# The output projection of a hybrid mixer block: three products of rounded and residual parts in place of one fp32 product

## The chip, the cores and the metric

The kernel runs on one core of a Trainium2 chip. The metric is the device time of one execution in microseconds. The inputs are fp32, and so is the output.

## What is computed

One block of a network over 512 rows of width 1024: a norm, a mixer, a residual; a second norm, a mixture of 32 experts, a residual. Cut to what matters here:

```
merged = g_sb * (y_sb @ w_o_sb) + g_rw * (y_rw @ w_o_rw)      # [512, 1024]
y  = merged @ w_out                                           # w_out [1024, 1024]
x  = x + gt1 * rmsnorm(y, norm_gains[l, 1])                   # x1
h  = rmsnorm(x, norm_gains[l, 2]) * (1.0 + sc2) + sh2
group_logits, expert_logits = h @ w_group, h @ w_router       # two experts a row
y  = sum over e of combine[:, e] * ((silu(h @ w_up1[e]) * (h @ w_up3[e])) @ w_down[e])
```

The change is in the second line, `merged @ w_out`.

## The kernel before, in words

Each engine has its own instruction stream, written out by hand, and the streams meet at counting semaphores. There is no planner: the order of the work is the order of the calls. All of SyncE's DMAs are on one queue. The work falls into stages:

- **Up to 544 us of the profile.** Modulation rows, the input projection, attention and the recurrent mixer. The first 15 tiles of the input projection (L1484 to L1486) are already computed as three products of rounded upper parts and lower parts in the type fp32r. Their upper parts are made by ScalarE (L661 for the weights, L673 for the rows), their lower parts by GpSimd (L520, L528) and VectorE (L1013).
- **Merging, 544 to 573.** TensorE makes eight tiles of the recurrent branch, each from four fp32 products (L1809, `mix_done`). VectorE multiplies each by its gate (L1199) and adds it to `merged` (L1200, `merged_ready`). `merged` is [128, 8, 512]: piece k holds 128 of the 1024 inner columns of all 512 rows, and lies in the first third of `ring`.
- **Output projection, 573 to 634.** `w_out` is loaded in two halves of 512 columns, WO1 first (into arena tiles 6 and 7), then WO0 (into the second third of `ring`). For each half TensorE goes over four tiles of 128 rows (t), each a sum over k of eight fp32 products 128x128 by 128x512: L1837 for WO1, L1847 for WO0, 32 products each. An fp32 product is two matmul records in the trace. A tile that is finished raises `y_done`. In the second half the transposes of finished rows (`transposes_x1`, L1819) and their router logits (`router_logits`, L1827) stand between the products of later tiles.
- **Behind each tile.** ScalarE squares and sums it (L866 for the first half, L870 for the second), takes the root (L872, L873), squares the row `x1` (L879 to L881), moves the transposed rows (L884), scales the row (L889) and stores it to DRAM (L890, `h2_stored`). VectorE makes `x1` (L1258, L1260, L1261, `x1_ready`). Ahead of the fourth tile of the second half VectorE also chooses experts for the first 256 rows (`choose(0)`, L1220 to L1248).
- **Routing, 634 to 661.** The last transposes and logits, the choice for the other rows, ranks and indices on VectorE with short products on TensorE, and some fp32 filler products (L1852). GpSimd then gathers the rows of the first experts (L563, `idx_ready`, `hrow_in`).
- **Experts, 661 to 1140.** 32 experts and some overflow blocks, 6 MB of weights each. Three sets of buffers are filled in turn by SyncE (L388 for `up`, L392 and L396 for `down`). Ahead of the loop, SyncE's list goes: at `merged_ready` = 8 it loads `down` of set 0 and, at `mix_done` = 32, both halves of `up` of set 1; at `y_done` = 4 `down` of set 1; at `y_done` = 8 both halves of `up` of set 0; at `x1_ready` = 8 one part of set 2 (L458, L459); and after `hrow_in[0]`, the landing of the first gather, the other part of set 2 (L464, L465), with which the loop follows. Each `load_expert(u, 0 or 1, e)` is two DMAs of 1 MB.

`S(i, n)` is n tiles of 2048 elements from tile i of the arena. `hT`, the transposed input rows, is S(15, 2), and is read last by the gate products ahead of 544.

Of the kernel before, what the change touches and what calls it, by code (L numbers as in the profile page):

```python
# [13 lines left out]
F32 = mybir.dt.float32  # L14
F32R = mybir.dt.float32r
I32 = mybir.dt.int32
ALU = mybir.AluOpType
# [3 lines left out]
P = 128  # L21
# [96 lines left out]
def build(nc, x, c, w_mod, b_mod, gains, w_in, gate_bias, shift_mu, w0, w_decay_up, a0, w_iclr_up, w_gate_up,  # L118
# [3 lines left out]
    with ctx:  # L122
        def sb(name, shape, dt=F32):
            return ctx.enter_context(nc.sbuf_tensor(name, shape, dt))
# [14 lines left out]
        with (nc.sbuf_tensor("w_parts", [P, 2, 2, KD, P], F32R) as w_parts,  # L139
              nc.sbuf_tensor("between0", [P, 2 * 4096 + 3 * 2048], F32), nc.sbuf_tensor("h_upper", [P, KD, T], F32R) as h_hi,  # L140
              nc.sbuf_tensor("between1", [P, 2048], F32), nc.sbuf_tensor("h_lower", [P, KD, T], F32R) as h_lo):
            pass
        ring = sb("ring", [P, 3, 4096])

        with nc.sbuf_tensor("below", [P, 10 * 2048], F32), nc.sbuf_tensor("sp_parts", [P, 4, ZW], F32R) as sp_parts:
# [29 lines left out]
        def S(i, n=1):  # L175
            return arena[:, i:i + n, :].rearrange("p a b -> p (a b)")
# [38 lines left out]
        acc_l += [rt[:, :], S(12, 1)[:, 1024:1536], S(12, 1)[:, 1536:2048]]  # L215

        y_late = S(2, 1).rearrange("p (t n) -> p t n", t=NT)
        y_early = S(13, 1)[:, 0:1024].rearrange("p (b n) -> p b n", b=2)
        squares = S(12, 1)[:, 1024:2048]
        shift_wr = rt[:, 0:KD * (NG + E)].rearrange("p (k n) -> p k n", k=KD)  # L220
        shift_row = rt[:, 470:470 + NG + E]
        h2tok = S(5, 1).rearrange("p (b n) -> p b n", b=2)
# [141 lines left out]
        def arrived(eng, name):  # L364

            n = chunk_names.index(name)
            eng.wait_ge(ring_in[slot_of[n]], 16 * slot_of[:n + 1].count(slot_of[n]))
# [44 lines left out]
        def _(sp):  # L412
# [32 lines left out]
            load_expert(sp, 0, 2, 0)  # L445
            sp.wait_ge(mix_done, 4 * KD)
            load_expert(sp, 1, 0, 1)
            load_expert(sp, 1, 1, 1)
            sp.wait_ge(y_done, NT)
            load_expert(sp, 1, 2, 1)  # L450
            sp.wait_ge(y_done, 2 * NT)
            load_expert(sp, 0, 0, 0)
            load_expert(sp, 0, 1, 0)
            first = lambda i, m: esrc[i][:, bass.ds(2, 1), 2048 * m:2048 * m + 2048].rearrange("p a n -> p (a n)")
            first_down = dn[:, bass.ds(2, 1), :, :].rearrange("p a k n -> p (a k) n")
            sp.wait_ge(x1_ready, 2 * NT)
# [59 lines left out]
        def _(pool):  # L516
# [32 lines left out]
            for n in range(KD):  # L549
                pool.wait_ge(osb_evac, n + 1)  # L550
                nc.gpsimd.tensor_tensor(merged[:, n, :], merged[:, n, :], osb[:, n % 2, :], ALU.mult).then_inc(sb_gated, 1)

            pool.wait_ge(merged_ready, KD)
            nc.gpsimd.memset(S(14), 0.0)
            nc.gpsimd.memset(S(13)[:, D:2 * D], 0.0).then_inc(hrow_zero, 1)
# [57 lines left out]
        def _(act):  # L613
# [246 lines left out]
            gate_evac(6)  # L860
            gate_evac(7)
            nc.scalar.preload_act_table_set("natural_log_exp_and_others")

            for t in range(NT):
                act.wait_ge(y_done, t + 1)
# [81 lines left out]
        def _(dve):  # L947
# [244 lines left out]
            ins.then_inc(yrw_ready, 1)  # L1192
            dve.wait_ge(yrw_ready, 1)

            dve.wait_ge(sb_gated, KD)
            for n in range(KD):
                dve.wait_ge(gr_evac, max(n + 1, 6))
                dve.wait_ge(mix_done, 3 * KD + n + 1)
                link(TT(gated[:, n % 2, :], gates_rw[:, n, :], ps[:, n % 4, :], ALU.mult))  # L1199
                TT(merged[:, n, :], merged[:, n, :], gated[:, n % 2, :], ALU.add).then_inc(merged_ready, 1)  # L1200
            dve.wait_ge(rows_moved, 80)
            dve.wait_ge(x_in, 32)
            for t in range(NT):
# [46 lines left out]
            for t in range(NT):  # L1250
                if t == NT - 1:
                    dve.wait_ge(rstd2, 2)
                    logits_out(0)
                    link(logits_out(1))
                    choose(0)
                dve.wait_ge(half_squared, NT + t + 1)
                y = y_early[:, t % 2, :]
                link(TT(y, ps[:, 4 + t, :], rows[:, 0, 0:512], ALU.mult))  # L1258
                dve.wait_ge(rstd1, t + 1)
                STT(x1[:, t, 512:1024], y_late[:, t, :], V("rs", 4 + t), x1[:, t, 512:1024], ALU.mult, ALU.add).then_inc(x1_ready, 1)  # L1260
                STT(x1[:, t, 0:512], y, V("rs", 4 + t), x1[:, t, 0:512], ALU.mult, ALU.add).then_inc(x1_ready, 1)  # L1261
# [135 lines left out]
        def _(pe):  # L1397
# [431 lines left out]
                last.then_inc(logit_done, 1)  # L1829


            pe.wait_ge(merged_ready, KD)
            arrived(pe, "WO1")
            for t in range(NT):
                w = chunk("WO1", KD)
                for k in range(KD):
                    last = mm(ps[:, t, :], merged[:, k, P * t:P * t + P], w[:, k, :], start=(k == 0), stop=(k == KD - 1))  # L1837
                last.then_inc(y_done, 1)
            arrived(pe, "WO0")
            for t in range(NT):  # L1840
                w = chunk("WO0", KD)
                for k in range(KD):
                    if k == 2 and t >= 2:
                        router_logits(t - 2)
                    if k == 4 and t >= 1:
                        transposes_x1(t - 1)
                    last = mm(ps[:, 4 + t, :], merged[:, k, P * t:P * t + P], w[:, k, :], start=(k == 0), stop=(k == KD - 1))  # L1847
                last.then_inc(y_done, 1)
            def idle_products(count):

                for _ in range(count):
                    mm(ps[:, 1, :], K("ones"), cst[:, 0:512], start=True, stop=True, skip_group_check=True)  # L1852
# [134 lines left out]
```

## Time and profile before

| | us |
|---|---|
| median of 3 runs | 1174.03 (1172.61 to 1175.0) |
| profiled execution, its own time | 1173.3 |
| its span, first to last instruction | 1171.1 |
| TensorE busy | 1034.2 (88%) |
| VectorE, ScalarE, GpSimd busy | 384.3, 259.9, 170.7 |
| mean granted TensorE clock | 0.975 |
| moved by DMA | 281.64 MB, mean 240 GB/s |

The durations in the rows come from the one profiled execution. Times in the rows are us from the first instruction, or ns where a group gives a mean. "PE" is TensorE's products, "PEld" its loads of the stationary operand, DVE is VectorE, ACT ScalarE, POOL GpSimd and SPq the queue that SyncE issues. Matmul ends are modelled, so the distance from start to start is what a product costs, and not the duration of one record. The granted clock is 1.00 at 2.4 GHz and 0.50 at 1.2 GHz.

### The profile page before, as it was taken

Reading aid. Unit: us, or ns where it says so; the run is one execution under the profiler, and the core shown is the slowest. Engines: PE = TensorE matmul, PEld = TensorE weight load, DVE = VectorE, ACT = ScalarE, POOL = GpSimd, SP = SyncE. Lnnn points to the kernel's source line nnn. Section 1 sums busy time; section 2 is a strip of 40 time slices with the busy share of each in tenths; the row PEclk is TensorE's granted clock in tenths of the full one; section 3 lists DMA queues with packets and bytes.
Section 4 is the critical chain, followed back from the end, with each engine's and each line's share of the span. In section 5 each row is a group of like instructions: output and inputs, shape, how many; then the busy total and the mean of one; then the engine's idle time right before and its main releaser. Section 6 shows DMA issues by size and latency. Waiting matters only on the chain.

```text
span 1171.1 us, 16601 instructions
## 1 busy us (share of the span) xinstructions
PE 1034.2 (88%) x6906; PEld 516.8 (44%) x6906; DVE 384.3 (33%) x810; ACT 259.9 (22%) x407; POOL 170.7 (15%) x222
## 2 busy tenths in 40 slices
PE   3899999999998999999999799987778777887886
PEld 1578644466555676544446333332233332332231
DVE  1322566465547442114215521221111111111114
ACT  2342350075552222233024000000000000000004
POOL 0345100003320100000100112111111111011002
PEclk9699999999999999999999899999999999899998
DMA  8444304443321002325334899999999999999995
GB/s 327 151 135 134 130 14 143 144 144 109 108 82 63 3 4 76 109 76 213 154 133 169 313 400 403 401 391 411 406 404 409 406 406 409 392 399 401 412 412 224
DMA packets 71184, 281.64 MB, mean 240 GB/s; under 512 B 9754, under 2 KB 19244, under 8 KB 46554
## 3 DMA queue, kind: packets, MB, share of 16 engines
q1 hardware_dynamic: 63408, 265.94, 58.7%
q0 software_dynamic: 5120, 8.40, 2.2%
q10 hardware_dynamic: 2602, 6.52, 1.5%
q8 instruction: 42, 0.69, 0.2%
q14 instruction: 12, 0.10, 0.0%
HBM read 276.62 MB, written 12.60 MB: 247 GB/s over the span
## 4 chain that ended last, share of the span: by engine, by line
PE 51%; SPq 30%; DMA 7%; DVE 5%; ACT 4%; issue 2%; POOL 1%; ACTq 0%; POOLq 0%; DVEq 0%
SPq L388 21%; PE ps L1590 7%; SPq L392 5%; PE ps L1471 5%; PE ps L1901 4%; SPq L396 3%; PE ps L1601 2%; PE ps L1484 2%; DMA ring<-in_w_up 2%; PE ps L1485 2%; PE ps L1486 2%; PE ps L1837 2%; PE ps L1847 2%; PE ps L1809 2%; PE ps L1516 2%
## 5 line engine op out<-in xcount | busy, mean ns | idle before, releaser
L1901 PE MATMUL ps<-arena 128*64 128x512 f32 x672 | 151.7, 596 | 31.9 <-DMA arena<-in_w_up 31.9
L1357 DVE TENSOR_TENSOR arena<-arena,ps 128x256 f32<-128x256 f32 x32 | 13.5, 421 | 372.1 <-ACT arena L904 372.1
L1590 PE MATMUL ps<-arena,ring 128*128 128x512 f32 x256 | 118.6, 604 | 0.2 <-DMA ring<-in_w_in 0.2
L1901 PEld LDWEIGHTS ps<-arena 128*64 128x64 f32 x672 | 48.6, 137 | 133.4 <-issue 101.9
L1916 PE MATMUL ps<-arena 128*64 128x512 f32 x336 | 79.9, 618 | 20.0 <-DMA arena<-in_w_down 15.3
L1901 PE MATMUL ps<-ring,arena 128*64 128x512 f32 x352 | 80.5, 603 | 18.9 <-DMA ring<-in_w_up 18.7
L904 ACT ACTIVATE arena<-ps 128x256 f32<-128x256 f32 x32 | 12.3, 383 | 260.9 <-PE ps L1901 260.9
L1590 PEld LDWEIGHTS ps<-arena,ring 128*128 128x128 f32 x256 | 46.1, 190 | 49.0 <-issue 47.2
L1352 DVE TENSOR_SCALAR arena<-ps,par 128x64 f32<-128x64 f32 x256 | 67.1, 333 | 0.5 <-PE ps L1890 0.5
L911 ACT ACTIVATE arena<-ps 128x512 f32<-128x512 f32 x32 | 19.1, 597 | 187.9 <-PE ps L1916 187.9
L536 POOL TENSOR_SCALAR_AFFINE_SELECT arena<-arena 128x128 f32<-128x128 f32 x64 | 32.3, 537 | 186.4 <-DVE arena L1092 168.6
L1901 PEld LDWEIGHTS ps<-ring,arena 128*64 128x64 f32 x352 | 24.2, 138 | 74.2 <-issue 42.1
L1916 PE MATMUL ps<-ring,arena 128*64 128x512 f32 x176 | 46.7, 680 | 10.7 <-DMA ring<-in_w_down 8.3
L1471 PE MATMUL ps<-arena,ring 128*128 128x512 f32 x128 | 55.1, 592 | 0.0
L1916 PEld LDWEIGHTS ps<-arena 128*64 128x64 f32 x336 | 25.5, 142 | 60.0 <-issue 43.0
L1484 PE MATMUL ps<-h_upper,w_parts 128*128 128x512 f32 (+1 forms) x120 | 47.9, 399 | 4.4 <-ACT arena L669 4.4
L520 POOL TENSOR_TENSOR w_parts<-ring,w_parts 128x1024 fp32r<-128x1024 f32 (+1 forms) x15 | 38.6, 2577 | 79.8 <-ACT w_parts L661 79.8
L589 POOL COPY dst_now<-dst_i 128x1 int32 x27 | 4.8, 177 | 300.2 <-ACT arena L911 300.2
L1485 PE MATMUL ps<-h_lower,w_parts 128*128 128x512 f32 (+1 forms) x120 | 47.7, 398 | 0.0
L1486 PE MATMUL ps<-h_upper,w_parts 128*128 128x512 f32 (+1 forms) x120 | 47.6, 397 | 0.0
L1890 PEld LDWEIGHTS ps<-cst,arena 64*128 64x128 f32 x256 | 30.7, 200 | 28.5 <-issue 28.5
L1471 PEld LDWEIGHTS ps<-arena,ring 128*128 128x128 f32 x128 | 24.3, 190 | 30.6 <-issue 30.6
(354 smaller groups left out, 1472.2 us busy)
## 6 DMA issues: line engine op xcount, KB each, us to landing
arena<-in_w_up SPq DMA_DIRECT2D x84, 1024.0 KB, 28.8
ring<-in_w_up SPq DMA_DIRECT2D x44, 1024.0 KB, 28.5
ring<-in_w_down SPq DMA_DIRECT2D x11, 2048.0 KB, 34.8
arena<-in_w_down SPq DMA_DIRECT2D x11, 2048.0 KB, 32.1
ring<-in_w_mod SPq DMA_DIRECT2D x10, 2048.0 KB, 9.1
arena<-in_w_down SPq DMA_DIRECT2D x20, 1024.0 KB, 28.2
ring<-in_w_in SPq DMA_DIRECT2D x6, 2048.0 KB, 8.4
ring<-in_w_in SPq DMA_DIRECT2D x8, 1024.0 KB, 9.0
```

The costliest lines, as they stand in the source:

```text
L388: eng.dma_start(eset_up[u][i][:, 2048 * m:2048 * m + 2048], src).then_inc(w_in_sem[u][m], 16)
L392: eng.dma_start(dst, src).then_inc(w_in_sem[u][m], 16)
L396: eng.dma_start(eset_down[u][i], src[:, i, :]).then_inc(w_in_sem[u][m], 16)
L520: nc.gpsimd.tensor_tensor(w_parts[:, n % 2, 1, :, 0:w], chunk(name, KD)[:, :, a:a + w], w_parts[:, n % 2, 0, :, 0:w].bitcast(F32), ALU.sub ...
L1352: last = TS(hgT[:, k, :], ps[:, 0, CAP * k:CAP * k + CAP], V("A1", k), V("SH1", k), ALU.mult, ALU.add)
L1471: last = mm(ps[0:m_, b, :], w[:, k, a:a + m_], hT[:, k, :], start=(k == 0), stop=(k == KD - 1))
L1484: mm(ps[0:m_, b, :], hi, h_hi[:, k, :], start=(k == 0), stop=False)
L1485: mm(ps[0:m_, b, :], hi, h_lo[:, k, :], start=False, stop=False)
L1486: last = mm(ps[0:m_, b, :], lo, h_hi[:, k, :], start=False, stop=(k == KD - 1))
L1590: last = mm(ps[:, bank, :], w[:, k, P * (n % 2):P * (n % 2) + P], hT[:, k, :], start=(k == 0), stop=(k == KD - 1))
L1901: last = mm(ps[64 * hf:64 * hf + 64, UP_BANK[u], :].rearrange("p (m n) -> p m n", m=2), hgT[:, k, :], up_pair(u, k)[:, :, 256 * hf:256 * h ...
L1916: last = mm(ps[64 * hf:64 * hf + 64, DOWN_BANK[u], :], hv2[:, k % 2, k // 2, :], wd[:, k % 2, 512 * hf:512 * hf + 512], start=(k == 0), st ...
```

## The change

The 64 fp32 products of the output projection become 192 products of the type fp32r: for each piece k and each row tile, upper part of `merged` by upper part of `w_out`, lower part of `merged` by upper part of `w_out`, upper part of `merged` by lower part of `w_out`. ScalarE makes the upper parts (a copy to fp32r), GpSimd the lower parts of the weights, VectorE those of `merged`. The lower parts overwrite what they come from. The upper parts of WO1 lie in `hT`, those of WO0 in arena tiles 9 and 11, those of `merged` in tiles 0, 1 and 13. Tiles 9 and 11 are the second half of `up` of set 1, so its load goes behind `y_done` = 8. TensorE no longer waits for all of `merged` ahead of the first product, but for each piece's parts in the first row tile of each half. Lines of the diff that only declare are kept where the text speaks of them.

```diff
@@ build: storage (element counts per partition, 4 bytes each)
+        with (nc.sbuf_tensor("over0", [P, 4096], F32), nc.sbuf_tensor("wo0_lower", [P, KD, 512], F32R) as wo0_lower,
+              nc.sbuf_tensor("over1", [P, 4096 + 1024], F32), nc.sbuf_tensor("m_upper0", [P, 6, 512], F32R) as m_upper0,
+              nc.sbuf_tensor("over2", [P, 7 * 2048], F32), nc.sbuf_tensor("wo0_upper0", [P, 4, 512], F32R) as wo0_upper0,
+              nc.sbuf_tensor("over3", [P, 2048], F32), nc.sbuf_tensor("wo0_upper1", [P, 4, 512], F32R) as wo0_upper1,
+              nc.sbuf_tensor("over4", [P, 2048], F32), nc.sbuf_tensor("m_upper1", [P, 2, 512], F32R) as m_upper1,
+              nc.sbuf_tensor("over5", [P, 3072], F32), nc.sbuf_tensor("wo1_upper", [P, KD, 512], F32R) as wo1_upper):
+            pass
-        y_early = S(13, 1)[:, 0:1024].rearrange("p (b n) -> p b n", b=2)
+        y_early = [a[:, :, :].rearrange("p b n -> p (b n)") for a in (SAs, SDZ)]
+        m_hi = [m_upper0[:, k, :] for k in range(6)] + [m_upper1[:, k, :] for k in range(2)]
+        m_lo = [w_parts[:, :, :, :, :].rearrange("p a b k n -> p (a b k n)")[:, 512 * k:512 * k + 512] for k in range(KD)]
+        wo_hi = [[wo1_upper[:, k, :] for k in range(KD)],
+                 [wo0_upper0[:, k, :] for k in range(4)] + [wo0_upper1[:, k, :] for k in range(4)]]
+        wo_lo = [[h_lo[:, k, :] for k in range(KD)], [wo0_lower[:, k, :] for k in range(KD)]]
@@ block.sync
             load_expert(sp, 1, 0, 1)
-            load_expert(sp, 1, 1, 1)
             sp.wait_ge(y_done, NT)
             load_expert(sp, 1, 2, 1)
             sp.wait_ge(y_done, 2 * NT)
             load_expert(sp, 0, 0, 0)
             load_expert(sp, 0, 1, 0)
+            load_expert(sp, 1, 1, 1)
@@ block.gpsimd, ahead of pool.wait_ge(merged_ready, KD)
+            def output_weight_lower(half, k):
+                pool.wait_ge(w_rounded, len(proj_tiles) + KD * half + k + 1)
+                nc.gpsimd.tensor_tensor(wo_lo[half][k], chunk(("WO1", "WO0")[half], KD)[:, k, :], wo_hi[half][k].bitcast(F32), ALU.subtract).then_inc(w_split, 1)
+            for k in range(KD):
+                output_weight_lower(0, k)
+            for k in range(KD):
+                output_weight_lower(1, k)
@@ block.scalar, ahead of the first act.wait_ge(y_done, t + 1)
+            def output_weight_upper(half, k):
+                A(wo_hi[half][k], chunk(("WO1", "WO0")[half], KD)[:, k, :], ACT.Copy).then_inc(w_rounded, 1)
+            arrived(act, "WO1")
+            for k in range(KD):
+                output_weight_upper(0, k)
+                act.wait_ge(merged_ready, k + 1)
+                A(m_hi[k], merged[:, k, :], ACT.Copy).then_inc(h_rounded, 1)
+            arrived(act, "WO0")
+            for k in range(KD):
+                if k == 4:
+                    act.wait_ge(mix_done, 4 * KD)
+                output_weight_upper(1, k)
@@ block.vector, the loop that makes merged
+            def merged_lower(k):
+                dve.wait_ge(h_rounded, KD + k + 1)
+                TT(m_lo[k], merged[:, k, :], m_hi[k].bitcast(F32), ALU.subtract).then_inc(h_split[1], 1)
                 TT(merged[:, n, :], merged[:, n, :], gated[:, n % 2, :], ALU.add).then_inc(merged_ready, 1)
+                if n:
+                    merged_lower(n - 1)
+            merged_lower(KD - 1)
-                y = y_early[:, t % 2, :]
+                y = y_early[t % 2]
@@ block.tensor
-            pe.wait_ge(merged_ready, KD)
-            arrived(pe, "WO1")
+            def output_products(half, t, k):
+                if t == 0:
+                    pe.wait_ge(h_split[1], KD // 2 + k + 1)
+                    pe.wait_ge(w_split, len(proj_tiles) + KD * half + k + 1)
+                at, bank = slice(P * t, P * t + P), 4 * half + t
+                mm(ps[:, bank, :], m_hi[k][:, at], wo_hi[half][k], start=(k == 0), stop=False)
+                mm(ps[:, bank, :], m_lo[k][:, at], wo_hi[half][k], start=False, stop=False)
+                return mm(ps[:, bank, :], m_hi[k][:, at], wo_lo[half][k], start=False, stop=(k == KD - 1))
             for t in range(NT):
-                w = chunk("WO1", KD)
+                pe.wait_ge(merged_ready, KD // 2 + t + 1)
                 for k in range(KD):
-                    last = mm(ps[:, t, :], merged[:, k, P * t:P * t + P], w[:, k, :], start=(k == 0), stop=(k == KD - 1))
+                    last = output_products(0, t, k)
                 last.then_inc(y_done, 1)
-            arrived(pe, "WO0")
             for t in range(NT):
-                w = chunk("WO0", KD)
                 for k in range(KD):
                     if k == 2 and t >= 2:
                         router_logits(t - 2)
                     if k == 4 and t >= 1:
                         transposes_x1(t - 1)
-                    last = mm(ps[:, 4 + t, :], merged[:, k, P * t:P * t + P], w[:, k, :], start=(k == 0), stop=(k == KD - 1))
+                    last = output_products(1, t, k)
                 last.then_inc(y_done, 1)
```

## Rows read from the trace of the kernel before

**Rows 1.** The page, part 2: 40 slices of 29.3 us each.

```profile
PE   3899999999998999999999799987778777887886
...
PEclk9699999999999999999999899999999999899998
DMA  8444304443321002325334899999999999999995
```

**Rows 2.** The chain that ended last: start us, us, what.

```profile
543.99 27.48 PE ps L1809 x64
573.03 27.73 PE ps L1837 x64
...
657.09 3.70 DMA arena<-h_rows,idx_i
...
1096.42 28.21 DMA ring<-in_w_up
```

**Rows 3.** Timeline, 572 to 601: start us, us, engine, line, operation.

```profile
573.03 27.73 PE L1837 MATMUL ps<-arena,ring 128*128 128x512 f32 x64 [1.57 <-DVE ring L1200]
...
573.57 0.19 PEld L1837 LDWEIGHTS ps<-arena,ring 128*128 128x128 f32 x1 [0.24 <-issue]
...
600.18 0.19 PEld L1847 LDWEIGHTS ps<-ring 128*128 128x128 f32 x1 [0.24 <-issue]
```

**Rows 4.** Timeline of TensorE, 87 to 100: input projection, three products a step.

```profile
87.94 0.39 PE L1486 MATMUL ps<-h_upper,w_parts 128*128 128x512 f32 x1
...
99.50 0.39 PE L1486 MATMUL ps<-h_upper,w_parts 128*128 128x512 f32 x1
```

**Rows 5.** Windows: us, busy time of each engine, granted clock, DMA share, GB/s.

```profile
50.50:54.90 4.40, 4.40 (x11) 3.37 (x11) 1.66 (x3) 0.70 (x2) 1.28 (x1) 0.50 0.00 0
...
650.00:655.00 5.00, 1.60 (x30) 1.60 (x32) 4.51 (x20) 0.00 (x0) 0.00 (x0) 0.76 1.00 423
655.00:660.00 5.00, 4.08 (x12) 1.38 (x8) 4.11 (x17) 0.89 (x1) 2.31 (x3) 0.56 0.16 48
```

**Rows 6.** Groups by line, whole span, shapes apart: busy, mean ns.

```profile
L1200 DVE TENSOR_TENSOR ring<-ring,arena 128x512 f32<-128x512 f32 x8 | 5.5, 691 | 0.3
...
L528 POOL TENSOR_TENSOR h_lower<-arena,h_upper 128x512 fp32r<-128x512 f32 x4 | 5.2, 1302 | 4.1 <-ACT h_upper L673 4.1
...
L673 ACT ACTIVATE h_upper<-arena 128x512 fp32r<-128x512 f32 x8 | 4.6, 622 | 0.1
```

**Rows 7.** Timeline, 47 to 49: VectorE and GpSimd side by side.

```profile
47.07 1.39 POOL L528 TENSOR_TENSOR h_lower<-arena,h_upper 128x512 fp32r<-128x512 f32 x1 [0.58 <-ACT h_upper L673]
...
47.54 1.47 DVE L1013 TENSOR_TENSOR h_lower<-arena,h_upper 128x512 fp32r<-128x512 f32 x1 [0.20 <-ACT h_upper L673]
```

**Rows 8.** Timeline, 607 to 636: the second half's products, and what follows them.

```profile
607.67 0.60 ACT L870 ACTIVATE arena<-ps 128x512 f32<-128x512 f32 x1 [5.85 <-PE ps L1847]
...
609.79 0.75 DVE L1261 SCALAR_TENSOR_TENSOR arena<-arena,par 128x512 f32<-128x512 f32 x1
...
614.25 0.35 ACTq L890 DMA_DIRECT2D h_rows<-arena  x1
...
628.37 0.26 DVE L1220 SCALAR_TENSOR_TENSOR arena<-ps,par,rt 128x36 f32<-128x36 f32 x1 [0.40 <-PE ps L1827]
...
633.48 0.23 DVE L1248 TENSOR_TENSOR arena<-arena 128x64 f32<-128x64 f32 x1
...
634.47 2.11 SPq L388 DMA_DIRECT2D ring<-in_w_up  x4
...
634.47 0.60 ACT L870 ACTIVATE arena<-ps 128x512 f32<-128x512 f32 x1 [1.38 <-PE ps L1847]
...
635.19 0.69 DVE L1258 TENSOR_TENSOR arena<-ps,arena 128x512 f32<-128x512 f32 x1 [1.49 <-ACT arena L870]
```

**Rows 9.** Line L563, the gathers of rows: issues and landing.

```profile
L563 POOL DMA_INDIRECT arena<-h_rows,idx_i x5: 936/951/1146, 657.1 to 1082.1; - x5
...
DMA to landing us min/median/max: 3.7/7.2/8.5
```

## The prediction

> **What bounds the kernel now.** I read the slices first. TensorE is busy nearly throughout, and the DMA share lies at 9 tenths from the 24th slice on, while in the 13th to the 22nd it is 5 tenths at most [rows 1]. So the kernel has two parts with different limits. The chain of waits says the same: up to about 650 us it goes through TensorE's products, the output projection's among them, and then over the first gather, which takes 3.70 us, into a long run of weight transfers whose last one lands at 1124.6 [rows 2]. What stands ahead of that run and on the chain moves the end by its full length; what makes the experts' arithmetic faster would not.
>
> At the start of the output projection the timeline shows a wait of 1.57 us: TensorE could begin at 571.46, and begins at 573.03, when the last piece of `merged` is there [rows 3]. Then its loads follow each other without a pause at the full clock: from the third, at 573.57, to the first of the second half, at 600.18, are 62 steps [rows 1, 3].
>
> **Products.** An fp32 product is two records. One record costs (600.18 - 573.57) / 62 = 0.429 us, one product 0.858, and 64 of them 54.9 us [rows 3]. The new form is in the trace already, in the input projection: 51 products of type fp32r, of the same shape, start between 87.94 and 99.50, so one costs 11.56 / 51 = 0.2267 us [rows 4]. 192 of them are 43.5 us. The sum gains **11.4 us**, all on the chain. The 0.39 us that a record shows is its modelled duration, with its neighbours overlapped; the starts decide.
>
> The Trainium skill, "TensorE: Matmul & The Clock Gate", section "Wait — 56ns, not 53.3ns?", gives 215.7 ns from start to start for 512 columns at the warm clock; that would make 192 products 41.4 us and the gain 2.1 us larger. The trace has 226.7 for this very type and shape, and that is used.
>
> **The wait ahead of them.** The new list lets TensorE start once five pieces are merged, and asks for each piece's parts only when it comes to it. It starts at 571.46: **1.6 us** more. Is the last piece ready in time? It is needed after 21 products, at 571.46 + 21 x 0.2267 = 576.2. `merged` is complete at 573.0. ScalarE's rounding takes 0.62 and VectorE's subtraction 0.69 [rows 6], so 574.3. If GpSimd works beside it, a subtraction takes 1.47 in place of 0.69 [rows 7], so 575.1. Both fit, by 1.1 us at least, and I cost it at nothing.
>
> **The weights' parts.** For WO1, ScalarE has 2 x 0.62 us of work per piece of `merged`, and pieces come every 27.48 / 8 = 3.4 us [rows 2, 6]. VectorE's work per piece goes from 1.4 to 2.1 us, or 2.8 beside GpSimd, under the same cover. GpSimd needs 1.30 to 1.39 us each [rows 6, 7]; its eighth starts two roundings behind the seventh merged piece, at 569.6 + 1.2 = 570.8, and ends at 572.2, four microseconds ahead of need. For WO0, ScalarE rounds eight pieces from 573.7 to 578.7; behind them wait only its sums of squares, the first due at 576.9, which has until the second half to be done. GpSimd's eight subtractions, from 574.3 on, end by 574.3 + 11.1 = 585.4. The second half starts at 571.46 + 96 x 0.2267 = 593.2. The cover is 8 us deep; without it 11.1 us would lie on TensorE's path. GpSimd's clearing of buffers, behind these, is not needed before the gather.
>
> **The second half's tiles.** Two chains ran here beside slower products, and must be checked. ScalarE's chain for one tile runs from 607.67 to 614.60, 6.9 us [rows 8]. A tile of products now takes 24 x 0.2267 = 5.4, with about 0.9 of transposes 6.3, and in the last two tiles some 1.7 of router logits on top. So the second tile's sum starts 0.6 late, and this is regained in the third. The transposes come 12 products, 2.7 us, behind a tile, and the rows they need come 2.2 and 2.9 behind it (607.67 to 609.79, and 0.75 more) [rows 8]; the one needed last has four transposes of cover. VectorE's choice for the first rows runs from 628.37 to 633.7, and the first instruction behind it starts at 635.19 [rows 8]: 1.5 us of slack. It is released inside the fourth tile, behind which six pieces are left; they shrink by 6 x (0.858 - 0.680) = 1.1 us. 0.4 us of slack remains. I cost all this at nothing, with a bound of 1.5 us.
>
> So everything from the last tile on comes 11.4 + 1.6 = **13.0 us** earlier.
>
> **The moved load.** Two DMAs of 1 MB leave a place, at 573, where the DMA has time, for the stretch behind the last tile, and on SyncE's queue they stand behind the loads of set 0 and ahead of set 2's and of the wait for the gather. Two more issues delay set 2's by about 1 us, which nobody waits for. At 423 GB/s, 2.1 MB are 5.0 us of stream. The stream from 634.47 on ends near 655 before, and then the DMA is nearly idle until the gather has landed, at 660.8 [rows 2, 5, 8]. The new stream ends 5.0 us later against the stage, near 660; the gather is issued at 657.1, so it falls within the last 2.9 us of it, where it had the DMA for itself. The gather's landing takes 3.7 us in idle DMA (its minimum) and 7.2 in the median, most of them under load [rows 9]. The delay is thus between 0 and 3.5 us. The overlap is about half of what a gather in full load sees, so I take the middle, **1.8 us**. The resumption of the stream waits for that landing, so this is lost at the end as well; the 5.0 us itself is not, since it fills idle time.
>
> By the Trainium skill, "DMA: Bandwidth & Descriptors", section "Queues, rings and completion order", each DMA engine alternates between queues packet by packet. A gather of 64 rows of 4 KB would then take only its own 0.6 us twice, and the sum would be 1.2 us lower. The median landing under load is 3.5 us longer, so more than taking turns stands behind it here.
>
> **The sum.** The profiled execution took 1173.3 us. 1173.3 - 13.0 + 1.8 = 1162.1. It lies 0.7 below the median of the three runs, which spread over 2.4; I put the forecast between the two footings, at **1162.4**.
>
> **Rivals.**
> 1. *The hidden things are not hidden.* The load's move costs the full 3.5, and one of the chains of the second half (ScalarE, choice) or the piecewise start gives 1.5 to 3 us of waits. For it: slacks of 0.4 and 1.1 us are thin, and waits at every piece are new. Against: each was priced with margin. 1173.3 - 13.0 + 3.5 + 1.5 to 3 = 1165.3 to 1166.8. Chance 0.15.
> 2. *The stream absorbs the gain* (no change). If the transfers from 573 on were one unbroken run, an earlier projection would only lengthen a wait further on. Against: the DMA is nearly idle from 655 to 660 [rows 5], and mostly unused during the projection [rows 1]. The time would be 1173 to 1175. Chance 0.05.
> 3. *Slower: the clock.* At half clock ten fp32r products start in 4.40 us, 0.44 each [rows 5], which is more than a third of an fp32 product at full clock. Three products beat one only while their mean is below 0.858 / 3 = 0.286 us, and with the 1.6 and 1.8 counted about the same. If the denser mix of loads and products, or a pause at the first piece, dropped the clock in this stage, 192 x 0.44 = 84.5 us against 54.9: 1173.3 + 29.6 - 1.6 + 1.8 = 1203; at a quarter of the products so slowed, 1173.3 - 11.2 + 48 x 0.213 = 1172, from where it turns. Against: the granted clock is 9 tenths or more in every slice but the second, the later products of this type included, and TensorE comes out of 30 us without a pause [rows 1, 2]. Chance 0.03.
> 4. *The form is not what it says*: fp32r products between these operands run as fp32 ones, 192 x 0.858, and the time is near 1280. The trace has one record for each such product, and a third of the cost [rows 4]. Chance 0.01.
>
> The forecast's own case, 1159.5 to 1164.5, has 0.76. It covers a landing delay of 0 to 3.5 us and both footings.
>
> **The numbers.** The range goes from 1159.0 (no delay, and the run-to-run spread) to 1167.0, the upper end of rival 1, and holds about 0.9; with doubt about my own bookings, 8 in 10. No measurement of this kernel tells a difference under 0.2% (2.3 us) from none. Faster by more: 0.91 (the own case and rival 1), within: 0.05 (rival 2), slower: 0.04 (rivals 3 and 4).
>
> **What the changed profile would show.** The first output product at 571.5 with no wait for VectorE; starts 0.227 us apart, granted clock 1.00; the first half over 21.8 us later, near 593; the last `y_done`, where SyncE issues set 0's `up`, at 621.4 in place of 634.5; the DMA in use without a gap up to the gather; the gather's landing at 5 to 6 us in place of 3.7, and at 648 to 650. From there to the end the same length as before. I would be wrong if products of the first row tiles wait for GpSimd or ScalarE, if VectorE's choice holds the last tile's `x1`, or if the expert stage takes longer than before although it starts earlier.

## The result, and the profile after

| | before | after |
|---|---|---|
| median, us | 1174.13 (1172.61 to 1175.0) | 1162.76 (1162.51 to 1165.32) |
| ratio | | 0.9909, 95% interval 0.9895 to 0.9923 |
| span of the profiled execution | 1171.1 | 1160.9 |
| TensorE busy | 1034.2 | 1021.3 |
| ScalarE, GpSimd busy | 259.9, 170.7 | 273.3, 190.9 |

The time falls by 11.4 us, 1.0%. The forecast was 1162.4, with a range of 1159.0 to 1167.0.

The page's slices, which answer to [rows 1]:

```profile
PE   3799999999998999999998699988787877778785
...
PEclk9799999999999999999999799999999999999999
DMA  9444304443322002315346999999999999999995
```

TensorE has 64 more matmul records and 13 us less work. The DMA's run of nines begins one slice earlier.

The timeline where the projection begins, TensorE first and then the other engines, answers to [rows 3]:

```profile
571.61 0.79 PE L1881 MATMUL ps<-wo_upper,m_upper 128*128 128x512 f32 x1
572.24 0.39 PE L1882 MATMUL ps<-wo_upper,w_parts 128*128 128x512 f32 x1
...
572.70 0.40 PE L1881 MATMUL ps<-wo_upper,m_upper 128*128 128x512 f32 x1
...
579.52 0.39 PE L1881 MATMUL ps<-wo_upper,m_upper 128*128 128x512 f32 x1
```

```profile
573.00 0.69 DVE L1240 TENSOR_TENSOR ring<-ring,arena 128x512 f32<-128x512 f32 x1
...
573.61 1.48 DVE L1233 TENSOR_TENSOR w_parts<-ring,m_upper 128x512 fp32r<-128x512 f32 x2
...
573.73 0.63 ACT L892 ACTIVATE m_upper<-ring 128x512 fp32r<-128x512 f32 x1 [2.28 <-DVE ring L1240]
...
574.27 4.26 ACT L886 ACTIVATE wo_upper<-ring 128x512 fp32r<-128x512 f32 x8
...
574.96 6.30 POOL L568 TENSOR_TENSOR wo_lower<-ring,wo_upper 128x512 fp32r<-128x512 f32 x5 [2.15 <-ACT wo_upper L886]
```

The first product follows the last one of the merging (the stage began 0.7 us later in this execution, which no part of the change touches), with no wait for VectorE. From 572.70 to 579.52 are 30 products: 0.2273 us each, against 0.2267 in [rows 4]. The last piece of `merged` is complete at 573.7, its parts at 575.1 (the two subtractions of VectorE from 573.61 are the seventh and the eighth). TensorE needs them after 21 products, at 576.8 by these starts, and does not stop.

The groups of the new work on the other engines (busy us, mean ns of one), which answer to [rows 6]:

```profile
L568 POOL TENSOR_TENSOR h_lower<-arena,wo_upper 128x512 fp32r<-128x512 f32 x8 | 10.2, 1270 | 108.6 <-ACT wo_upper L886 108.6
L568 POOL TENSOR_TENSOR wo_lower<-ring,wo_upper 128x512 fp32r<-128x512 f32 x8 | 10.0, 1293 | 2.2 <-ACT wo_upper L886 2.2
...
L1233 DVE TENSOR_TENSOR w_parts<-ring,m_upper 128x512 fp32r<-128x512 f32 x8 | 5.5, 684 | 0.1
L892 ACT ACTIVATE m_upper<-ring 128x512 fp32r<-128x512 f32 x8 | 5.0, 630 | 18.3 <-DVE ring L1240 18.3
...
L886 ACT ACTIVATE wo_upper<-ring 128x512 fp32r<-128x512 f32 x8 | 4.3, 616 | 0.0
```

None of it stands on the chain. ScalarE's eight roundings of WO0 follow each other from 574.27, GpSimd's subtractions from 574.96; the second half of the products begins at 594.

SyncE's queue and the first gather, as issues and as a piece of the chain:

```profile
573.72 0.38 SPq L404 DMA_DIRECT2D ring<-in_w_down  x1
...
593.99 0.38 SPq L404 DMA_DIRECT2D arena<-in_w_down  x1
622.11 2.56 SPq L400 DMA_DIRECT2D ring<-in_w_up  x4
624.71 1.30 SPq L400 DMA_DIRECT2D arena<-in_w_up  x2
...
651.60 0.80 SPq L476 DMA_DIRECT2D arena<-in_w_up  x2
...
660.47 4.64 SPq L400 DMA_DIRECT2D ring<-in_w_up  x4
```

```profile
644.74 6.78 DMA arena<-h_rows,idx_i
```

These rows give the stage lengths. SyncE issues at 573.72 when `merged` is complete, at 622.11 when the last output tile is: 48.39 us, where it was 573.01 to 634.47, 61.46 us. That is **13.07 us** less. The gather is issued 22.6 us behind the last tile, as before. Its landing takes 6.78 us against 3.70 [rows 2].

The slack of VectorE's choice and ScalarE's chain, which answer to [rows 8]:

```profile
622.14 0.23 DVE L1291 TENSOR_TENSOR arena<-arena 128x64 f32<-128x64 f32 x1
622.83 0.69 DVE L1301 TENSOR_TENSOR SDZ<-ps,arena 128x512 f32<-128x512 f32 x1 [0.46 <-ACT arena L905]
```

```profile
606.43 0.60 ACT L905 ACTIVATE arena<-ps 128x512 f32<-128x512 f32 x1 [0.43 <-ACT arena L924]
```

The choice ends at 622.37, and the next instruction waits 0.46 us for ScalarE. Only at the second tile does ScalarE go from one tile's chain into the next without waiting for TensorE (0.43 us behind its own last instruction); at the others it waits for the products.

### The profile page after: what moved, and what is told of

It reads as the page before. It is cut to its first block, busy times and chain, and to the rows that moved or that the text cites. A ratio compares the mean times of both kernels' runs of the same rounds, so it can differ in the third digit from the quotient of the medians.

```text
span 1160.9 us, 16792 instructions
## 1 busy us (share of the span) xinstructions
PE 1021.3 (88%) x6970; PEld 533.8 (46%) x6970; DVE 391.0 (34%) x818; ACT 273.3 (24%) x431; POOL 190.9 (16%) x238
## 4 chain that ended last, share of the span: by engine, by line
PE 52%; SPq 28%; DMA 7%; DVE 5%; ACT 4%; issue 2%; POOL 1%; ACTq 0%; POOLq 0%; DVEq 0%
SPq L400 20%; PE ps L1633 7%; SPq L404 5%; PE ps L1514 5%; PE ps L1951 5%; SPq L408 3%; PE ps L1966 3%; PE ps L1644 2%; DMA ring<-in_w_up 2%; PE ps L1527 2%; PE ps L1528 2%; PE ps L1529 2%; PE ps L1559 2%; PE ps L1852 2%; DMA ring<-in_w_mod 2%
## 5 line engine op out<-in xcount | busy, mean ns | idle before, releaser
L1951 PE MATMUL ps<-arena 128*64 128x512 f32 x672 | 151.7, 596 | 33.8 <-DMA arena<-in_w_up 33.8
L1966 PE MATMUL ps<-arena 128*64 128x512 f32 x336 | 83.5, 641 | 19.8 <-DMA arena<-in_w_down 15.1
L1951 PE MATMUL ps<-ring,arena 128*64 128x512 f32 x352 | 81.2, 605 | 17.2 <-DMA ring<-in_w_up 17.2
L1633 PEld LDWEIGHTS ps<-arena,ring 128*128 128x128 f32 x256 | 46.1, 190 | 49.0 <-issue 47.2
L1951 PEld LDWEIGHTS ps<-ring,arena 128*64 128x64 f32 x352 | 26.8, 139 | 70.0 <-issue 39.4
L1966 PE MATMUL ps<-ring,arena 128*64 128x512 f32 x176 | 41.7, 617 | 10.6 <-DMA ring<-in_w_down 8.2
L1940 PE MATMUL ps<-cst,arena 64*128 64x64 f32 x256 | 35.0, 278 | 6.0 <-DMA arena<-h_rows,idx_i 6.0
```

The lines of the kernel that those rows point to most:

```text
L1633: last = mm(ps[:, bank, :], w[:, k, P * (n % 2):P * (n % 2) + P], hT[:, k, :], start=(k == 0), stop=(k == KD - 1))
L1940: last = tr(ps[:, 0, CAP * k:CAP * k + CAP], hv[:, k, :], ident[0:CAP, 0:CAP])
L1951: last = mm(ps[64 * hf:64 * hf + 64, UP_BANK[u], :].rearrange("p (m n) -> p m n", m=2), hgT[:, k, :], up_pair(u, k)[:, :, 256 * hf:256 * h ...
L1966: last = mm(ps[64 * hf:64 * hf + 64, DOWN_BANK[u], :], hv2[:, k % 2, k // 2, :], wd[:, k % 2, 512 * hf:512 * hf + 512], start=(k == 0), st ...
```

## The experiments

All were compared with the kernel before in the same rounds. For each, the table gives the median and five lengths from SyncE's queue and the chain of its profiled execution: from `merged` complete to the last output tile; from there to the issue of the first gather; its landing; from its issue to the first release of a buffer by TensorE (the second time that `up` of set 0 is loaded); and from there to the end of the span.

| | median, us | projection | to gather | landing | issue to release | release to end |
|---|---|---|---|---|---|---|
| before | 1174.13 | 61.46 | 22.62 | 3.70 | 11.99 | 502.0 |
| changed | 1162.76 | 48.39 | 22.63 | 6.78 | 15.73 | 500.4 |
| changed, second job | 1161.74 | 48.39 | 22.63 | 7.47 | 15.87 | 500.7 |
| changed, third job | 1163.55 | 48.36 | 22.64 | 6.83 | 15.64 | 499.9 |
| E1 before, load moved | 1173.73 | 61.45 | 22.65 | 4.95 | 12.65 | 501.3 |
| E2 changed, no gather wait | 1163.62 | 48.41 | 22.61 | 7.92 | 15.86 | 500.4 |
| E3 before, no gather wait | 1178.62 | 61.46 | 22.65 | 8.47 | 16.35 | 500.9 |
| E4 changed, two products | 1152.62 | 36.12 | 25.76 | 3.82 | 11.89 | 501.3 |
| E5 changed, waits for all of `merged` | 1164.55 | 50.25 | 22.64 | 6.64 | 14.19 | 501.5 |
| E6 changed, 1 MB left early | 1160.26 | 48.38 | 22.62 | 3.63 | 11.90 | 501.7 |
| E6, third job | 1159.73 | 48.4 | 22.5 | 3.95 | 11.88 | 502.3 |
| E8 changed, load behind the gather | 1166.23 | 48.40 | 22.65 | 3.62 | 11.73 | 506.1 |

The second and third job are later sets of runs of the same kernel. The kernel before had medians of 1174.13 beside the changed kernel's first runs, 1173.67 beside E1, E2, E3 and the first E6, 1173.81 beside the second job, E4, E5 and E8, and 1174.78 in the third job. So medians from different jobs compare to about 1 us only; where that matters the ratio to the kernel before is given. The five lengths are of one execution each.

My first account was that the products gain 11.4 us and the start 1.6, that the moved load gives a part back through the first gather, and that behind the gather the weight stream bounds the end. Rivals: the gather is late for another reason; the stream, or TensorE, bounds alone.

### E1: only the load is moved

```diff
@@ block.sync of the kernel before
             load_expert(sp, 1, 0, 1)
-            load_expert(sp, 1, 1, 1)
...
             load_expert(sp, 0, 1, 0)
+            load_expert(sp, 1, 1, 1)
```

> The kernel before with one edit: the second half of the up weights of set 1 (2 MB) is loaded behind the eighth y_done, as in the changed kernel; products stay fp32. My theory: the moved 2 MB run beside the first gather, whose landing goes from 3.7 to about 6.8 us; the stream resumes 3.1 us later and the kernel takes about 1177 us (2 to 3.5 more than before). Rival: the place of the load costs nothing, the gather in the changed kernel is late for another reason; landing 3.7 us and time within 1 us of before.

The landing, and the first release on SyncE's queue:

```profile
657.30 4.95 DMA arena<-h_rows,idx_i
```

```profile
669.95 4.64 SPq L388 DMA_DIRECT2D ring<-in_w_up  x4
```

The landing is between the two expectations, 1.25 us longer than before; the release is 0.7 us later against the issue, and the time is the rival's, that of before: ratio 1.0003 (0.9994 to 1.0012). My theory, 2 to 3.5 us more, missed. So the move delays the gather, but less here than in the changed kernel, and here nothing of it is left at the end.

### E2 and E3: no wait for the gather

```diff
@@ block.sync, of the changed kernel (E2) and of the kernel before (E3)
             sp.wait_ge(h2_stored, 16 * NT)
-            sp.wait_ge(hrow_in[0], 16)
```

> The changed kernel without SyncE's wait for the first gather ahead of the second part of set 2. Theory A, the weight stream bounds everything from here on: the DMA time that is not used between 648 and 656 (about 3.3 us) comes back, less what a gather under full load adds; 1159.5 to 1162. Rival B, the gather's landing bounds (TensorE starts the experts with it, and the stream has slack): landing goes from 6.8 to 7 to 8.5 us and the time rises to 1163 to 1165.

> The kernel before without SyncE's wait for the first gather. Theory A (the stream bounds): the DMA is unused for about 6.5 us around that wait, so up to that much comes back: 1167 to 1171. Rival B (the gather's landing bounds): landing goes from 3.7 to 7 or more, and the time to 1177.

The gather, SyncE's queue and windows behind the landing (us, busy time of each engine, granted clock, DMA share, GB/s), E2 and then E3:

```profile
643.98 7.92 DMA arena<-h_rows,idx_i
```

```profile
637.39 0.80 SPq L475 DMA_DIRECT2D arena<-in_w_up  x2
...
659.84 4.64 SPq L400 DMA_DIRECT2D ring<-in_w_up  x4
```

```profile
652.00:654.00 2.00, 1.96 (x14) 1.88 (x15) 0.81 (x4) 0.00 (x0) 0.18 (x1) 0.50 0.95 274
...
658.00:660.00 2.00, 2.00 (x12) 1.29 (x10) 0.00 (x0) 0.00 (x0) 0.00 (x0) 1.00 0.94 334
```

```profile
656.80 8.47 DMA arena<-h_rows,idx_i
```

```profile
649.85 0.80 SPq L463 DMA_DIRECT2D arena<-in_w_up  x2
...
673.15 4.64 SPq L388 DMA_DIRECT2D ring<-in_w_up  x4
```

```profile
667.00:669.00 2.00, 2.00 (x16) 2.00 (x16) 1.68 (x7) 0.00 (x0) 0.99 (x1) 0.50 0.00 0
669.00:671.00 2.00, 2.00 (x11) 1.22 (x10) 0.00 (x0) 0.60 (x1) 0.00 (x0) 0.85 0.23 64
671.00:673.00 2.00, 2.00 (x12) 1.31 (x10) 0.00 (x0) 0.00 (x0) 0.00 (x0) 1.00 0.00 0
```

Theory A fell in both, and rival B held: in E2 within its range, in E3 with 1178.62 even above its 1177. In E2 the second part of set 2 goes out at 637.39 in place of 651.60, and the time is that of the changed kernel: ratio 0.9913 (0.9899 to 0.9926), where the changed kernel has 0.9909, 0.9890 and 0.9902. The DMA is at its full share from there on, but between 652 and 660 it moves only 274 to 365 GB/s beside the gathers. In E3 the landing goes to 8.47 us and the kernel becomes slower, ratio 1.004 (1.0027 to 1.0054). Its rows show why the early bytes are of no use: from 667 to the release at 673.15 next to nothing moves. All three sets of buffers are full, and the stream stands until TensorE frees a part, which it does one half of an expert behind the gather. **Up to the first release the gather's landing counts, and bytes brought forward don't.** E3 shows this; E2 only agrees, since neither effect shows in its time.

### E8: the moved load behind the gather

```diff
@@ block.sync of the changed kernel
             load_expert(sp, 0, 1, 0)
-            load_expert(sp, 1, 1, 1)
...
             sp.wait_ge(hrow_in[0], 16)
+            load_expert(sp, 1, 1, 1)
```

> The changed kernel with the moved 2 MB behind the landing of the first gather in place of ahead of it. Both theories: landing 3.7 us, the first expert 3 us earlier. Theory A, from there on the stream bounds by its bytes: 5.0 us more bytes, 3.1 us earlier start, 1164 to 1165. Theory C, the stream has slack up to the first release of a buffer by TensorE, since three sets are all that fit, and only the first expert's time counts: 1159.5 to 1160.5.

SyncE's queue:

```profile
646.45 3.62 DMA arena<-h_rows,idx_i
```

```profile
650.13 0.81 SPq L400 DMA_DIRECT2D arena<-in_w_up  x2
...
658.18 4.64 SPq L400 DMA_DIRECT2D ring<-in_w_up  x4
```

The landing is back at 3.62 us and the release comes 11.73 us behind the issue, 4 us sooner than in the changed kernel, and yet the median is 1166.23, above the 1164 to 1165 of theory A. The length from the release to the end is 506.1 us, against 501.3 to 502.3 in the other versions with an undisturbed landing (before, E4, E6) and 499.9 to 500.7 in the changed kernel. These 2 MB are 5.0 us of stream that are not done by the release; the length is 3.8 to 4.8 us above the former and 5.4 to 6.2 above the latter, so about all of them is paid. So theory A's mechanism holds from the first release on, and theory C, which would have the first expert's time alone count, is out. The 1.2 us by which the median is above theory A's range need no further cost here: in the profiled execution `merged` is complete 1.7 us later than in the changed kernel (575.40 and 573.72), ahead of everything that the edit touches. I have no cause for that. E3 and E8 together: **up to the release the gather counts, behind it the bytes not yet loaded.**

### E6: one of the two moved DMAs at its old place

The four upper parts of WO0 that lay in tile 11 go to tile 14, whose clearing for the gathered rows waits for the eighth `y_done`; tile 11 can be loaded at 574 again.

```diff
@@ storage
-              nc.sbuf_tensor("over3", [P, 2048], F32), nc.sbuf_tensor("wo0_upper1", [P, 4, 512], F32R) as wo0_upper1,
-              nc.sbuf_tensor("over4", [P, 2048], F32), nc.sbuf_tensor("m_upper1", [P, 2, 512], F32R) as m_upper1,
-              nc.sbuf_tensor("over5", [P, 3072], F32), nc.sbuf_tensor("wo1_upper", [P, KD, 512], F32R) as wo1_upper):
+              nc.sbuf_tensor("over3", [P, 3 * 2048], F32), nc.sbuf_tensor("m_upper1", [P, 2, 512], F32R) as m_upper1,
+              nc.sbuf_tensor("over4", [P, 1024], F32), nc.sbuf_tensor("wo0_upper1", [P, 4, 512], F32R) as wo0_upper1,
+              nc.sbuf_tensor("wo1_upper", [P, KD, 512], F32R) as wo1_upper):
@@ block.sync; up_part(i) is DMA i of load_expert(sp, 1, 1, 1)
             load_expert(sp, 1, 0, 1)
+            up_part(1)
...
             load_expert(sp, 0, 1, 0)
-            load_expert(sp, 1, 1, 1)
+            up_part(0)
@@ block.gpsimd
-            pool.wait_ge(merged_ready, KD)
+            pool.wait_ge(y_done, 2 * NT)
             nc.gpsimd.memset(S(14), 0.0)
```

> The changed kernel with the upper parts of the last four pieces of WO0 in arena tile 14 in place of 11 (its clearing waits for the eighth y_done), so that one of the two moved 1 MB loads can stand at its old place. Theory: the stream that meets the gather ends 2.5 us earlier, the gather lands in 3.7 to 4.5 us in place of 6.8, and the time is 1159.5 to 1160.5. Rival (the delay of the gather is not from the moved load): landing stays above 6 us, the time at 1162 to 1163.

The gather and SyncE's queue:

```profile
644.06 3.63 DMA arena<-h_rows,idx_i
```

```profile
574.47 0.52 SPq L458 DMA_DIRECT2D arena<-in_w_up  x1
...
647.77 0.81 SPq L481 DMA_DIRECT2D arena<-in_w_up  x2
...
655.96 4.64 SPq L400 DMA_DIRECT2D ring<-in_w_up  x4
```

The result is what my account expected: landing 3.63 us, release 3.8 us sooner against the issue, median 1160.26. The two intervals against before still touched (0.9872 to 0.9902, and 0.9895 to 0.9923), so the pair ran once more in common rounds.

> The changed kernel, beside the version with one load left early, on one chip and in the same rounds. 1161.7 to 1162.8; gather landing 6.5 to 7.5 us.

> The version with one of the two moved 1 MB loads at its old place, beside the changed kernel. If the moved load costs what its gather landing says (3.1 to 3.8 us late, part of it regained), 2 to 2.5 us less than the changed kernel: 1159.5 to 1160.5, landing 3.6 us. If the difference of the first comparison was chance: within 1 us of the changed kernel.

The changed kernel: 1163.55 (1162.45 to 1163.86), E6: 1159.73 (1159.24 to 1160.12); the ranges are 2.3 us apart. The changed kernel lay 0.75 us above what was expected of it, E6 within. So the second of the two moved MB costs the changed kernel 1.5 to 3.8 us by the three comparisons of medians (1161.74 and 1162.76 against 1160.26, and this pair); only the pair, with 3.8, ran in common rounds. E6 still has the other MB moved, and no run has both at their old place beside the new products. E6, with 0.9867 (0.9851 to 0.9884) against before, is the **fastest full version of the study**.

### The changed kernel again

> The changed kernel once more, as it is, beside the others of this batch. My account: gather landing 5 to 7 us after 22.6 us from the last output tile, time 1162 to 1163.5, and 2 to 3 us above the version with one load left early. If the landing of 6.8 us was chance, it comes out at 3.7 to 5 here, and the difference to that version has another cause.

The landing of 6.8 us was no chance: 7.47 here, 6.83 in the third job, 6.64 in E5. The median, 1161.74, lay a quarter of a microsecond below the range given, and 1.5 above E6's first median, short of the 2 to 3.

### E5: TensorE waits for all of `merged`

```diff
@@ block.tensor of the changed kernel
             for t in range(NT):
-                pe.wait_ge(merged_ready, KD // 2 + t + 1)
+                pe.wait_ge(merged_ready, KD)
```

> The changed kernel with TensorE waiting for all eight pieces of merged ahead of the first output product, as before the change. My booking: 1.6 us of idle TensorE come back, at the end too; 1164.0 to 1164.8. Rival: the last piece's parts held the first tile anyway, and 0 to 0.5 us come back.

TensorE's first output product:

```profile
572.66 0.50 PE L1881 MATMUL ps<-wo_upper,m_upper 128*128 128x512 f32 x1 [1.58 <-DVE ring L1240]
```

The wait is back with the length it had before, 1.58 us, and the projection is 1.86 us longer. The median is 1164.55, inside the range of my booking; the rival is out for the stage. At the end the loss is likely but less sharp: the ratio is 0.9915 (0.9900 to 0.9930), and 0.9890 (0.9875 to 0.9906) for the changed kernel in the same job.

Its release came 1.5 us sooner behind the gather's issue than in the changed kernel, with a landing of about the same length. The rows give the cause, the granted clock. From the landing to the release, the changed kernel and then E5:

```profile
651.52:660.47 8.95, 8.81 (x43) 6.62 (x45) 2.11 (x8) 0.60 (x1) 1.17 (x2) 0.64 0.92 321
652.16:659.71 7.55, 7.40 (x43) 5.91 (x45) 2.11 (x8) 0.60 (x1) 1.17 (x2) 0.76 0.92 330
```

The clock is the number ahead of the last two: 0.64 and 0.76 in the mean. It stands at 0.50 up to 658.01 in the changed kernel, 6.49 us behind the landing, and up to 655.82 in E5, 3.66 us behind it. An estimate: work that is done at half clock for 2.83 us longer ends 1.4 us later, and the length from landing to release is 8.95 and 7.55 us, 1.40 apart. The same holds for the other two executions of the changed kernel: 5.37 and 6.21 us at 0.50, 8.40 and 8.81 us from landing to release.

### E4: two products in place of three

This kernel leaves out the product of `merged`'s upper parts with the lower parts of `w_out`.

```diff
@@ block.tensor of the changed kernel, output_products
-                mm(ps[:, bank, :], m_lo[k][:, at], wo_hi[half][k], start=False, stop=False)
-                return mm(ps[:, bank, :], m_hi[k][:, at], wo_lo[half][k], start=False, stop=(k == KD - 1))
+                return mm(ps[:, bank, :], m_lo[k][:, at], wo_hi[half][k], start=False, stop=(k == KD - 1))
```

> The changed kernel without the third product (upper part of merged by lower part of w_out is left out, so 128 products in place of 192). Theory 1, products alone set the pace of this stage: 64 x 0.2267 = 14.5 us less, 1148.3. Theory 2, the first half gets its full 7.3 us, and in the second half ScalarE's 6.9 us a tile and VectorE's choice take over: another 2 to 4 us at most, with a wait for VectorE ahead of the fourth tile's row; 1151 to 1153.5.

The end of the second half, VectorE, ScalarE and TensorE:

```profile
611.47 0.60 ACT L905 ACTIVATE arena<-ps 128x512 f32<-128x512 f32 x1 [0.40 <-ACT arena L924]
...
612.57 0.23 DVE L1291 TENSOR_TENSOR arena<-arena 128x64 f32<-128x64 f32 x1
612.71 0.68 DVE L1301 TENSOR_TENSOR SDZ<-ps,arena 128x512 f32<-128x512 f32 x1
...
614.33 1.94 PE L1862 MATMUL ps<-cst,arena 128*128 128x128 f32 x8 [2.26 <-DVE arena L1303]
```

Theory 2 holds: 1152.62. SyncE's issues at 573.83 and 586.92 bound the first half: 13.1 us, against 20.3 (573.72 to 593.99) in the changed kernel. That is 7.2 us less, the 32 products' full 7.3. The second half gets only 5.1 us shorter of its 7.3, and 3.1 us come back ahead of the gather. Two chains hold the fourth row: the tile is done at 609.95, ScalarE starts on it at 611.47, behind its own last instruction, and VectorE follows at 612.71, when its choice is over. That is 2.8 us behind the tile, 0.7 in the changed kernel (622.11, 622.83), and the transposes wait for the row (2.26 us). By these rows ScalarE's chain is the next bound, and VectorE's choice lies half a us behind it. The gather lands in 3.82 us here, since it comes 3.1 us later behind the same stream. Of 14.5 us the kernel keeps 9 to 10 by the medians (1152.62 against 1161.74 in the same job, and 1162.76), and the shorter landing is part of these.

## Why the prediction was right

Against the profiled execution of before, the span changed by -10.2 us: +0.7 up to the merging, which no part of the change touches; -13.07 in the projection; +3.74 from the gather's issue to the first release; -1.59 from there to the end.

- **Products, 11.4 us.** Right. The step of 0.2267 us taken from the input projection was 0.2273 here, and E4's first half returned 7.2 us for 32 products. The 215.7 ns of the Trainium skill ("TensorE: Matmul & The Clock Gate", section "Wait — 56ns, not 53.3ns?") would, as an estimate, have put the 192 products 2.2 us too short; the measurement decides for the trace's row.
- **The start, 1.6 us.** Right, and shown by E5 for the stage: 1.86 us. The rest of the stage came out as booked: together 13.07, forecast 13.0.
- **The covers.** Right. The last piece's parts were ready 1.4 us behind the complete `merged`, the optimistic one of the two times given (574.3 against 573.0), with GpSimd starting its next piece only then. The slack of VectorE's choice was forecast at 0.4 us and is 0.46. E4 shows that ScalarE's chain and this choice, half a us apart, are what comes next. Busy times alone would not have shown it.
- **The moved load, 1.8 us.** This is the term that was mis-sized: "The overlap is about half of what a gather in full load sees, so I take the middle". The landing grew by 3.1 to 3.8 us, that is by the upper bound of 3.5 and a little more or less, to 6.8 to 7.5 us in place of the 5 to 6 named as a sign, and the release came 3.7 to 3.9 us later against the issue. Behind the release 1.3 to 2.1 us were regained, so that the profiled execution lost 2.2 us net against the 1.8 booked. That these two agree is luck: a larger loss and a regain that was not booked. Why there is a regain I can't say; the length from release to end varies by 2.4 us over the versions (E8 left out), and is short in the changed kernel, E2 and E3, where the release is late.
- **Taking turns.** By the rule of the Trainium skill ("DMA: Bandwidth & Descriptors", section "Queues, rings and completion order") the landing would, as an estimate, have taken 0.6 us more. With work on both queues it was 3.1 to 4.8 us more (changed kernel, E2, E3). The packets below show why the rule did not price it: for the first 3.3 to 4.4 us the gathers' queue moved nothing at all, where it starts after 1.84 us otherwise. From then on both queues move side by side in E2 and E3.
- **"The resumption of the stream waits for that landing, so this is lost at the end as well".** The loss was right for the changed kernel (E6), and its reason half wrong. E2 and E3 show that SyncE's wait is not what costs: without it the changed kernel is as fast and the kernel before slower. The landing counts because TensorE's first expert starts with it, and because three full sets are as far as the stream can go (E3's empty windows).
- **The rivals.** Rival 1 (1165.3 to 1166.8) had the full landing delay right and its other waits wrong. Rival 2 lay far off. Rival 3: the granted clock was 1.00 from 573 to 622. It fell to 0.50 behind the projection, at the gather, as it did before. Two of its readings were off, without weight for the outcome: in [rows 1] the clock is at 8 tenths in three later slices (the 23rd, 35th and 40th), none of them in the projection, and at half clock the products of the input projection start 0.427 us apart in the trace, not 0.44.

Why does the same move delay the landing by 1.25 us in E1 and by 3.1 to 3.8 in the changed kernel? The traces keep every DMA packet with its queue. The table has, in us behind the issue of the first gather, when SyncE's queue ran dry (all but its last three packets), when the gathers' queue moved its first packet, and the landing; and what the gathers' queue had moved by then.

| | SyncE's queue dry | gathers' first packet | landing | MB by then |
|---|---|---|---|---|
| before | -2.0 | 1.84 | 3.70 | 0.24 |
| E6, first and third job | 1.0, 1.6 | 1.84, 1.84 | 3.63, 3.95 | 0.22, 0.31 |
| E1 | 2.7 | 2.80 | 4.95 | 0.41 |
| changed, three executions | 3.7, 3.7, 3.4 | 3.42, 3.46, 3.31 | 6.78, 7.47, 6.83 | 0.62, 0.71, 0.66 |
| E2, E3 | not by then | 4.34, 4.36 | 7.92, 8.47 | 0.30, 0.58 |

Two things add up. The gathers' first packet goes 1.84 us behind the issue where SyncE's queue is dry by then, and about when it runs dry where that is later. In the changed kernel it runs dry 3.4 to 3.7 us behind the issue, where my prediction had 2.9 and E1 has 2.7: beside ScalarE's third store of rows, issued 0.65 us ahead of the stream (621.46, 622.11) and no longer 1.35 us (633.12, 634.47), SyncE's first packet goes 1.7 us behind its issue in place of 1.0. The rest is argued, not isolated: GpSimd issues the gathers for the second and third expert at 646.19 and 647.45, 1.45 and 2.71 us behind the first. The longer the first is held, the more of the others travels with it, and by its landing the queue has moved 0.62 to 0.71 MB in place of 0.22 to 0.31. From the first packet the landing takes 1.8 to 2.1 us in before and E6, 2.15 in E1 and 3.4 to 4.0 in the changed kernel.

## What to carry to other kernels

Price a new form of a product by the distance of its starts in a part of the same kernel that uses it already, and then go through each engine that paced itself by the slower products: its slack shrinks by what the products lose. Where new storage forces a load to move, look for the small latency-bound transfer that it will meet, and give up as little of its old place as the storage allows: 1 MB less in its way was worth 1.5 to 3.8 us here. A prefetch stream that is bounded by its bytes later on may be bounded by its buffers now; bytes brought forward count only as far as there is room for them.

## What the runs showed of the hardware that was not expected

A gather of 64 rows of 4 KB that lands in 3.6 to 4.0 us with little else in the DMA took 7.9 and 8.5 us with the weight stream beside it (E2, E3), and already 6.6 to 7.5 us where the stream's queue ran dry 3.4 to 3.7 us behind its issue. It does not share from the start: its first packet goes when the stream's queue is dry, or after 4.36 us at the latest in these runs. And it does not lose only that wait: gathers issued behind it catch up. These are the changed kernel's windows around it (us, busy time of each engine, granted clock, DMA share, GB/s):

```profile
573.00:622.00 49.00, 49.00 (x247) 41.34 (x245) 15.53 (x39) 23.19 (x51) 13.15 (x11) 1.00 0.39 151
640.00:644.70 4.70, 3.64 (x35) 2.75 (x36) 4.00 (x15) 0.00 (x0) 0.00 (x0) 0.64 1.02 429
648.00:651.60 3.60, 0.00 (x0) 0.00 (x0) 1.11 (x2) 0.06 (x1) 1.40 (x2) 0.50 0.91 219
651.60:656.00 4.40, 4.34 (x27) 3.90 (x29) 2.11 (x8) 0.38 (x1) 1.17 (x2) 0.50 0.81 268
```

The first window is the projection, at the full clock. Ahead of the gather the DMA moves 429 GB/s. Between 648 and 651.6 its share is still 0.91, but only 219 GB/s move, and E2's windows show the same: with gathers on the way a share above 0.9 goes with half to four fifths of the bytes. TensorE, which has nothing to do from 648 to 651.6, is granted 0.50 there and on into the first expert, up to 658.0; by E5's comparison the length of that stretch alone moves the first release by 1.4 us.
